# Second half of the output projection ended tile by tile over held weights, first expert-retrieval head computed by tile, keys loaded straight to their place

## What is computed

```python
for i in range(DEPTH_2):                 # 2 layers; mixer 0 is an SSD, mixer 1 a retention
    hn = rms_norm_2(h, mix_norm[i])
    y = ...mixer...                      # ends in  y @ w_out,  2048 -> 1024
    h = h + y
    h = h + peer_ffn(rms_norm_2(h, ffn_norm[i]), peer_w_q[i], peer_keys[i], peer_u[i], peer_v[i])
    g = jax.nn.sigmoid(rms_norm_2(h, ple_norm[i]) @ ple_gate[i])
    h = h + g * (p[i] @ ple_proj[i])

def peer_ffn(h, w_q, sub_keys, u, v):    # K = 16, 8 heads
    q = (xt @ w_q).reshape(T, PEER_HEADS, 2, PEER_HALF)
    sc = jnp.einsum('thcd,hckd->thck', q, sub_keys)      # 2 x 128 scores per position and head
    s1, i1 = lax.top_k(sc[:, :, 0], K)
    s2, i2 = lax.top_k(sc[:, :, 1], K)
    cand = (s1[..., :, None] + s2[..., None, :])         # 256 sums, the best 16 are taken
    ...
    hid = gelu(einsum('tkd,td->tk', u[ib], xb))
    out = einsum('tk,tkd->td', gb * hid, v[ib])
```

## Time and profile before

| | us |
|---|---|
| median of 3 runs | 2423.48 |
| lowest and highest | 2421.09, 8536.05 |
| the profiled execution, its own time | 2424.95 |
| its span, first to last instruction | 2423.2 |
| PE busy | 2109.7 (87%) |
| DVE busy | 1728.3 (71%) |
| ACT busy | 785.4 (32%) |
| POOL busy | 612.1 (25%) |
| share of the chain that ended last: PE, DMA, DVE | 22%, 18%, 16% |
| moved by DMA | 726.67 MB |

### The profile page before, as it was taken

The page is one execution under the profiler, slowest core; times in us unless marked ns, Lnnn a source line. Parts: engine busy times, 40 slices in busy tenths (PEclk is TensorE's granted clock), DMA queues, the critical chain, the costliest instruction groups (busy, mean ns, idle before and its releaser), DMA issues.

```text
span 2423.2 us, 27837 instructions
## 1 busy us (share of the span) xinstructions
PE 2109.7 (87%) x9126; PEld 1373.9 (57%) x9126; DVE 1728.3 (71%) x3706; ACT 785.4 (32%) x1443; POOL 612.1 (25%) x520
## 2 busy tenths in 40 slices
PE   7999899999999789887878788999888988777777
PEld 7998789989877444332322237977544432222224
DVE  5555665558765787878787876646878887877786
ACT  4334653346574222211211116334411211211114
POOL 0000000000100455543434430000245544443440
PEclk9999999999999899999999999999999999999999
DMA  6554325554324999999999994544799999999995
GB/s 249 188 186 172 129 90 189 185 179 165 127 99 166 417 413 412 418 413 411 414 420 410 410 421 180 188 139 144 303 420 420 408 412 420 420 409 419 400 421 210
DMA packets 101195, 726.67 MB, mean 300 GB/s; under 512 B 11616, under 2 KB 11744, under 8 KB 13280
## 3 DMA queue, kind: packets, MB, share of 16 engines
q0 software_dynamic: 74016, 539.00, 54.1%
q1 hardware_dynamic: 25200, 181.41, 20.9%
q10 hardware_dynamic: 1872, 4.88, 0.6%
HBM read 724.21 MB, written 1.05 MB: 299 GB/s over the span
## 4 chain that ended last, share of the span: by engine, by line
PE 22%; DMA 18%; DVE 16%; issue 13%; ACT 2%; POOL 1%; DVEq 0%; POOLq 0%; ACTq 0%; SPq 0%
PE bank L1870 22%; DMA arena<-in_uv,expert 18%; DVE arena L1748 3%; DVE arena L1798 2%; POOL arena L623 1%; DVE arena L1725 1%; DVE arena L1721 1%; DVE sel_i L1727 1%; ACT w_hi L677 1%; DVE arena L1691 1%; DVE top_i L1699 1%; DVE lw_rounded L1158 1%; DVE top_i L1689 1%; DVE top_v L1694 1%; DVE top_v L1686 1%
## 5 line engine op out<-in xcount | busy, mean ns | idle before, releaser
L1870 PE MATMUL bank<-arena 128*128 128x512 f32 (+4 forms) x2416 | 1070.7, 577 | 252.5 <-DVE arena L1748 245.7
L623 POOL DMA_INDIRECT arena<-in_uv,expert x512 | 601.4, 1175 | 1146.2 <-PE bank L1870 606.9
L1870 PEld LDWEIGHTS bank<-arena 128*128 128x128 f32 (+2 forms) x2416 | 419.2, 193 | 827.2 <-DVE arena L1748 516.7
L1798 DVE SCALAR_TENSOR_TENSOR arena<-arena,xn 128x1024 f32<-128x1024 f32 x512 | 627.0, 1225 | 221.0 <-DMA arena<-in_uv,expert 206.2
L1158 DVE TENSOR_TENSOR lw_rounded<-lw,w_hi 128x2048 fp32r<-128x2048 f32 x169 | 389.4, 2306 | 221.0 <-ACT w_hi L677 217.8
L1060 ACT ACTIVATE act_h<-hid 128x1 f32<-128x1 f32 x512 | 103.3, 203 | 1018.5 <-DVE arena L1798 1018.1
L1870 PE MATMUL bank<-xT_hi,w_hi 128*128 128x256 f32 x1352 | 416.9, 308 | 6.8 <-DVE xT_lo L1199 6.8
L677 ACT ACTIVATE w_hi<-lw 128x2048 fp32r<-128x2048 f32 x169 | 323.3, 1917 | 274.2 <-PE bank L1870 237.4
L1870 PE MATMUL bank<-xT_hi,lw_rounded 128*128 128x256 f32 x1352 | 382.7, 283 | 0.0
L1870 PE MATMUL bank<-xT_lo,w_hi 128*128 128x256 f32 x1352 | 382.7, 283 | 0.0
L1870 PEld LDWEIGHTS bank<-xT_hi,w_hi 128*128 128x128 f32 x1352 | 258.7, 191 | 28.1 <-issue 25.1
(11 more groups left out here) (248 smaller groups left out, 1486.1 us busy)
## 6 DMA issues: line engine op xcount, KB each, us to landing
lw<-in_units SPq DMA_DIRECT2D x171, 1024.0 KB, 4.7
arena<-in_uv,expert POOLq DMA_INDIRECT x512
wide<-in_wide POOLq DMA_DIRECT2D x2, 1024.0 KB, 10.7
gain<-in_gains ACTq DMA_DIRECT2D x4, 512.0 KB, 7.2
h<-in_x SPq DMA_DIRECT2D x2, 512.0 KB, 5.8
arena<-in_ret_consts ACTq DMA_DIRECT2D x1, 1024.0 KB, 4.8
out<-xn SPq DMA_DIRECT2D x2, 512.0 KB, 2.6
consts<-in_consts ACTq DMA_DIRECT2D x1, 592.5 KB, 5.5
```

The lines of the kernel that those rows point to most:

```text
L623: nc.gpsimd.indirect_dma_start(out=rows_uv[:, slot, :], out_offset=None, in_=table, in_offset=bass.IndirectOffsetOnAxis(ap=expert[par][:, ...
L1798: V.scalar_tensor_tensor(rows_uv[:, slot, 0:D], rows_uv[:, slot, 0:D], 1.0, xn[:, tile, :], ALU.mult, ALU.mult, accum_out=hid[par][:, k:k ...
L1870: return nc.tensor.matmul(o, lhsT, rhs, start=start, stop=stop, **more)
```

## The change

1. **Projection.** In the second column half the first unit is used by both tiles; tile 0 then runs through the other three units alone, and these stay held until tile 1 has used them. Between two k-steps of tile 1 (`TURN_FIRST`) PE transposes tile 0 of the normalised rows. Norm, transpose and split go by tile.
2. **First head by tile.** Its query product for one tile has 24 matmuls of 256 columns, with x as the stationary side; the rows are copied, turned by PE, copied and scored. DVE's pick reads tile 0's scores from PSUM. The zeroing of banks 0 to 3 stands behind tile 0's first scores, tile 1 follows. Two heads are early now, and head 2 moves beside the gathers.
3. **Keys.** SP loads them by DMA into `wide`, when the mixer's gains in it have been read (`grp_ready`). They take no slot of the ring; the ACT copy is gone.

```diff
-EARLY_HEADS = 3
+EARLY_HEADS = 2
-HEAD_AT = {3: 4, 4: 20, 5: 36, 6: 52, 7: 68}
+HEAD_AT = {2: 1, 3: 13, 4: 25, 5: 40, 6: 56, 7: 72}
+TURN_FIRST = 9
-WHOLE = (A_PEER0, A_PEER1)
+WHOLE = (A_PEER0 + 1, A_PEER1 + 1)
@@ SP
-                load_units(loaded, first)
+                head = (A_PEER0, A_PEER1)[layer]
+                load_units(loaded, head)
+                sp.wait_ge(grp_ready, 8 * (layer + 1))
+                sp.dma_start(wide[:, :], units_d[head]).then_inc(keys_loaded, 16)
+                load_units(head, head + 1, 1)
+                load_units(head + 2, first)
@@ ACT group_turn
-                split((A_PEER0, A_PEER1)[m] + 2)
+                split((A_PEER0, A_PEER1)[m])
+                n = (N_PEER0, N_PEER1)[m]
+                square_root_table(n)
+                root_tile(n, 0)
+                split((A_PEER0, A_PEER1)[m] + 1)
+                high_tile(n, 0)
+                root_tile(n, 1)
@@ ACT peer
+                def first_query(t):
+                    if t == 0:
+                        act.wait_ge(q_done, layer + 1)
+                    else:
+                        act.wait_ge(lw_used, first + 2)
+                    copy(q_rows[:, t, :], bank[(0, 7)[t]][:, 0:2 * KEYS]).then_inc(q_copied, 1)
+                    act.wait_ge(q_turned, NT * layer + t + 1)
+                    ins = copy(pqT[:, 0, :, t * P:(t + 1) * P], ...)
+                    ins.then_inc(q_ready, 1)
+                first_query(0)
+                split(first + 3)
+                high_tile(n, 1)
+                first_query(1)
+                act.wait_ge(score_done, 8 * layer + 1)
+                copy(score[:, PEER_HEADS, :], bank[6][:, 2 * KEYS:4 * KEYS]).then_inc(score_act, 1)
                 split(first + 4)
-                for i in range(EARLY_HEADS):
+                softmax_exp(0)
+                for i in range(1, EARLY_HEADS):
@@ DVE group_out
-                add_last((E_SSD, E_RET)[m], ...)
+                split(end)
+                dve.wait_ge(first_tile, (E_SSD, E_RET)[m] + 1)
+                add_to_h([(TURN_BANKS[m][2], 0, BANK)])
+                scale_tile(n, 0)
+                split(end + 1)
+                low_tile(n, 0)
+                dve.wait_ge(lw_used, end)
+                add_to_h([(TURN_BANKS[m][3], 1, BANK)])
+                scale_tile(n, 1)
@@ DVE peer
-                split(first_unit + 3)
-                dve.wait_ge(score_act, 9 * layer + 1)
-                    link(V.tensor_copy(st[:, 0], score[:, 0, :]...))
+                    dve.wait_ge(first_scores, layer + 1)
+                    V.tensor_copy(st[:, 0], bank[6][:, 0:2 * KEYS]...).then_inc(first_read, 1)
                     ...
                     experts(early, EARLY_ROWS).then_inc(expert_early, 1)
-                    split(first_unit + 4)
+                    low_tile((N_PEER0, N_PEER1)[layer], 1)
+                    split(first_unit + 3)
                     ...
                 weigh(0, 0)
+                split(first_unit + 4)
@@ PE group_out, second half
+                for k in range(4):
+                    for t in range(NT):
+                        ins = out(t, k, w)
+                ins.then_inc(lw_used, 1)
+                held = []
+                for k in range(4, 16):
+                    if k % 4 == 0:
+                        held.append(out_unit())
+                    ins = out(0, k, held[-1])
+                ins.then_inc(first_tile, 1)
+                for k in range(4, 16):
+                    if k == TURN_FIRST:
+                        turn_tile((N_PEER0, N_PEER1)[m], 0)
+                    ins = out(1, k, held[k // 4 - 1])
+                    if k % 4 == 3:
+                        ins.then_inc(lw_used, 1)
@@ PE peer
+                def first_query(t):
+                    for k in range(KD):
+                        if k % HALF_KD == 0:
+                            pe.wait_ge(tile_dve, 2 * TILE_NO[n, t] + k // HALF_KD + 1)
+                        ins = product(bank[(0, 7)[t]][:, 0:2 * KEYS], both(xT, ...), both(w, ALL, k, ALL), ...)
+                    if t == 0: ins.then_inc(q_done, 1)
+                    else:      ins.then_inc(lw_used, 2)
+                    pe.wait_ge(q_copied, NT * layer + t + 1)
+                    ...two transposes, q_turned; wait q_ready; for t == 0 wait keys_loaded; two score products...
+                first_query(0)
+                for b in range(4):
+                    mm(bank[b][:, :], zeros, consts[:, 0:BANK], True, True).then_inc(slot_free, SLOTS // 4)
+                turn_tile(n, 1)
+                first_query(1)
-                for i in range(EARLY_HEADS):
+                for i in range(1, EARLY_HEADS):
```

More of the change, by code:

```diff
@@ L163 @@
 UNITS = A_PLE1 + U_PLE
-WHOLE = (A_PEER0, A_PEER1)
+WHOLE = (A_PEER0 + 1, A_PEER1 + 1)
+LOADS = {u: sum(v not in WHOLE for v in range(u % RING, u + 1, RING)) for u in range(UNITS)}
 SPLIT_UNITS = [u for u in range(UNITS) if u not in WHOLE]
@@ L576, in load_units @@
                 turns = (end - first) // RING
[L577 to L580, removed]
+                if turns:
+                    with sp.Fori(0, turns) as i:
+                        for u in range(first, first + RING):
+                            sp.wait_ge(lw_used, RING * i + (u - RING + 1))
+                            load_unit(RING * i + u, u % RING, stored)
                 for u in range(first + turns * RING, end):
@@ L1638, in experts @@
                         return V.scalar_tensor_tensor(expert[0][:, at], sel_i[:, 0, at], float(KEYS), sel_i[:, 1, at], ALU.mult, ALU.add)
-                    link(V.tensor_copy(st[:, 0], score[:, 0, :].rearrange("p (c k) -> p c k", c=2)))
+                    dve.wait_ge(first_scores, layer + 1)
+                    V.tensor_copy(st[:, 0], bank[6][:, 0:2 * KEYS].rearrange("p (c k) -> p c k", c=2)).then_inc(first_read, 1)
+                    dve.wait_ge(first_read, layer + 1)
                     for c in range(2):
@@ L1855, in _ @@
             ssd()
-            norm(N_PEER0)
             peer(0)
@@ L2155, in group_out, with out, out_unit @@
                 arriving[0] = (yT_dve, 8 * m)
[L2156 to L2160, removed]
[L2161 to L2165 removed]
+                steps = row_steps([(bank[TURN_BANKS[m][t]][:, :], t, 0, BANK) for t in range(NT)], srcT, (4, 4, 4, 4), BANK)
+                for g in (2, 3):
+                    for _ in range(4):
+                        next(steps)
+                    turn(g)
+                for _ in steps:
+                    pass
+                outs = [bank[TURN_BANKS[m][2 + t]][:, :] for t in range(NT)]
+                def out(t, k, w):
+                    return product(outs[t], both(srcT, ALL, k, slice(t * P, (t + 1) * P)), both(w, ALL, k % 4, ALL), k == 0, k == 15)
+                def out_unit():
+                    return [a.rearrange("p (k n) -> p k n", n=BANK) for a in next_unit()]
+                w = out_unit()
+                for k in range(4):
[14 more added lines that the diff above has]
+                        ins.then_inc(lw_used, 1)
             def ssd():
```

78 lines of the change are left out of this document (40 added, 38 removed).

## The result

The changed kernel took 2432.12 us (median of 5, 2429.12 to 2434.31), the kernel before 2423.48: a ratio of 1.0037 (95% interval 1.0026 to 1.0048). It is slower by some 8.6 us, where 8.5 us less was predicted (2415, range 2405 to 2424). The profiled execution took 2434.31, span 2432.5. The hand-over came as early as predicted; the time went elsewhere.

The account below looks back on a forecast made before the run. The DMA engines were taken to bound both gather stages, so only an earlier start gains: 10.8 - 5.5 - 0.3 = 5.0 us in layer 0, 4.7 in layer 1, 9.7 off 2424.95, hence 2415 us (range 2405 to 2424).

Parts of the forecast that it names:

- The hand-over: From tile 0's last sum through the first pick to gather 1: gather 1 earlier by 10.8 us, layer 1 by 10.5.
- The projection's term: Second half of the projection: tile 0 needs 60 matmuls instead of 84, so its sum ends at 755.65, 5.6 us earlier.
- Rival B: Gather start less early (late weights, extra link) or ring runs thin: 2 to 3 us less per layer, 2420; chance 0.22.
- D: Hand-over to the gathers no earlier, as the pick waits for something unseen: 2425, no change; chance 0.03.
- The unit loads: Gather stage: six loads behind gather 1 instead of four, 2.2 MiB more through saturated DMA engines, costing 5.5 us per layer.
- Rival A: Gather stage: the extra loads cost nothing, so all 21.3 us come through: 2403.6; chance 0.08.
- The ring at the start: First gather slots: dots near 789.7, gather 9 near 799, 3 us ahead of need; 0.3 us per layer charged.
- rival C: First gather slots: PE at lower clock starves the ring, 2452; a loss beyond about 3 such slots; chance 0.07.
- the thin ring of rival B: Gather ring, slots 1 to 8 also carrying head 2's products: 2 to 3 us less per layer, 2420; chance 0.14.
- The sum: Both layers: 5.0 us gained in layer 0 and 4.7 in layer 1, together 9.7, giving 2415 us.
- No engine's speed inside the stage is worth anything, as long as the DMA engines never run dry: Gather stages: they end when their bytes have moved, 2.5 us per MiB, so gain comes only from an earlier start.
- Does the stage stay fed?: Check of the gather stage's start: 27 us of DMA work until 804, gather 9 near 799; 0.3 us per layer charged.

Follow-up runs that it names:

- Experiment 9: Kernel of experiment 1 with the out projection's last three units again multiplied for both tiles in turn: 2431.89 us, ratio 1.0039.
- experiment 8: Kernel of experiment 1 with each of the six weight units behind a layer's first gather loaded twice: 2443.92 us, ratio 1.0088.
- experiment 1: Changed kernel with VectorE's code moved by 4 instructions (eight satisfied semaphore waits), nothing else: 2414.49 us, ratio 0.9967 to the kernel before.

## Why the prediction was wrong

*The hand-over: right.* The projection's term (14.05 us from the first half's sum) is met. The pick's copy was put at 770.0 and came at 770.45, gather 1 at 775.0 and 775.59; 0.43 of both was already in the first half's sum. Experiment 9 gives the tile order alone its price. Rival B falls (tile 0's sum at 756.08, PE without a gap), and so does D.

*The unit loads: right.* SP issues six loads behind gather 1, and between its first and last gather a stage holds 6.29 MB of unit loads where it held 4.19, so 2.0 MiB more where the sum has 2.2. With the code at a good place the stages grew by 6.1 and 4.9 us, 5.5 on average as predicted; experiment 8 shows the rate. Rival A falls.

*The ring at the start: right, and with it rival C's fall.* First dot at 790.10 (predicted 789.7), gather 9 at 798.29 (799). The windows behind them:

```profile
788.00:792.00 4.00, 1.16 (x8) 0.97 (x8) 3.40 (x5) 2.30 (x4) 0.00 (x0) 1.00 1.01 428
792.00:796.00 4.00, 2.29 (x3) 1.18 (x4) 3.86 (x16) 0.20 (x1) 0.00 (x0) 0.53 1.01 426
796.00:800.00 4.00, 4.00 (x7) 1.49 (x6) 3.82 (x16) 0.41 (x2) 1.53 (x1) 0.61 1.02 426
800.00:804.00 4.00, 4.00 (x20) 2.56 (x19) 3.76 (x12) 0.20 (x1) 2.61 (x2) 1.00 1.01 420
```

TensorE stood idle for 4.28 us up to 793.71, and the granted clock then is near its lower level, 1.2 GHz (0.53 and 0.61 in these windows), for about two slots, fewer than the three from which C decides; it is 1.00 again from 800. The DMA share stays at 1, so the thin ring of rival B did not come either.

*The sum: near, for the work.* The kernel of experiment 1 takes 2414.49 where 2415 was predicted. That the two agree to 0.5 us is partly luck: the prediction took its 9.7 us off one profiled execution of 2424.95, and against the median of the kernel before beside it, 2423.07, the work gained 8.6 us. By its trace layer 0's last gather goes out at 1433.39, 4.1 us earlier (predicted 5.0); layer 1's at 2361.49, 10.6 earlier (9.7). One reading was off and decided nothing: in the earlier trace rows the slices of the stages behind slice 24 go down to 400, with 303 and 210 at the edges, and the slices elsewhere run from 90.

*What failed* is the step "No engine's speed inside the stage is worth anything, as long as the DMA engines never run dry", with its check under "Does the stage stay fed?", which looked at the first 30 us only. The condition was broken twice per run, 500 us further on, by something that none of the edits does: VectorE's code had become eight instructions longer ahead of a loop. The sum had no term for that: 2432.12 - 2414.49 = 17.6 us, about 9 per jump, since the 14.6 us of POOL's idle time are partly covered by gathers in flight. Nor did a rival hold it, so the range ended 8 us below the result.

Could it have been foreseen? In part. The page of before shows the instruction queues, the built program the length of each loop, and both together that layer 0's loop was two pages and four instructions long: 3 places in 128 put it on a fourth page (10 for layer 1's). The price wasn't to be had from the trace of before, which has no such jump with a fetch behind it, and where a page begins is only known from these runs. An eight-instruction move had a chance of some 13 in 128 to land one of the loops there. A rival with a chance of 0.1 would have been fair, though its price came only from these runs.

## What to carry to other kernels

When a change moves the time the wrong way and each of its terms is met in the trace, look for idle time that ends with "issue" at a loop's jump back, and compare the packets of the instruction queues with the kernel before. Then move the code by a few instructions, with nothing else changed. Before a verdict on any edit that changes an engine's instruction count ahead of a loop, this cheap experiment tells the edit's worth from the luck of its place. A loop whose length is just above a whole number of code pages is worth placing on purpose or shortening; a loop written out is safe, but here it cost 6.4 us against a well-placed one.

## What the runs showed of the hardware

- A jump back of VectorE in a loop of 260 or 267 instructions costs nothing visible while the loop lies on three pages of 128 instructions (0.25 us from the branch to the next instruction), and some 11 us of standstill when it lies on four (11.0 in layer 0; 5.61 + 3.90 in layer 1), with five pages of 8 KiB fetched per turn. One instruction more or less decides.
- Under saturated DMA engines the later pages come every 5.0 us, twice a gather's 2.5; a packet itself takes 0.33 us. VectorE goes on 1.75 to 1.97 us behind the start of a page's packet in all ten stalling jumps. With the DMA engines idle at the jump the first wait is 2.5 to 2.7 us, against 6.1 with them saturated; with one gather under way in the second wait the standstill is still 6.8 to 7.0 us.
- 2 MiB of weights more per gather stage cost 4.9 to 6.1 us, 12 MiB more cost 29.4: bytes add up at 2.45 us per MiB.
